# Attention in a two-layer block on one core: inverse row sums applied to the results instead of to the probability tiles

## The reference, cut to what matters

```python
probs = jax.nn.softmax(scores, axis=-1).astype(v.dtype)
out = jnp.einsum('bhcqk,bckhd->bcqhd', probs, vb)
```

## Time and profile before

| | us |
|---|---|
| median of 3 runs | 1671.91 |
| lowest, highest | 1671.36, 1674.05 |
| the profiled execution | 1673.98 |
| its span | 1671.2 |
| TensorE busy in the span | 1641.2 |
| VectorE, ScalarE, GpSimd busy | 959.7, 670.5, 156.5 |

### The profile page before, as it was taken

One profiled execution on the slowest core, in us unless ns is written; L12 is line 12 of the kernel. 1 busy time (PEld: TensorE's weight loads), 2 busy tenths in 40 slices (PEclk: granted clock), 3 DMA queues, 4 the chain that ended last, 5 costly groups with the idle time before them and its releaser, 6 DMA issues.

```text
span 1671.2 us, 20833 instructions
## 1 busy us (share of the span) xinstructions
PE 1641.2 (98%) x8516; PEld 1386.0 (83%) x8516; DVE 959.7 (57%) x1406; ACT 670.5 (40%) x1036; POOL 156.5 (9%) x230
## 2 busy tenths in 40 slices
PE   7999999999999999999999999999999999999998
PEld 6879997788888888889998887888888888888787
DVE  6755668764242434645844558544557736745757
ACT  5523365543231413523673146541334414414444
POOL 0000016300000000002720037100000000000000
PEclk9999999999999999999999999999999999999999
DMA  5221131122222222223112220322222222222331
GB/s 184 76 84 68 51 126 51 40 87 101 100 84 95 101 101 101 103 107 119 52 51 101 80 88 36 126 101 101 101 96 93 101 101 101 100 84 94 117 110 51
DMA packets 25614, 153.17 MB, mean 92 GB/s; under 512 B 3504, under 2 KB 5936, under 8 KB 8368
## 3 DMA queue, kind: packets, MB, share of 16 engines
q1 hardware_dynamic: 23184, 145.52, 24.4%
q10 hardware_dynamic: 2336, 6.33, 1.0%
HBM read 147.65 MB, written 4.19 MB: 91 GB/s over the span
## 4 chain that ended last, share of the span: by engine, by line
PE 88%; DVE 6%; ACT 2%; issue 2%; POOL 1%; DMA 0%; POOLq 0%; SPq 0%; DVEq 0%; ACTq 0%
PE bank L524 23%; PE bank L525 23%; PE bank L526 23%; PE bank L534 3%; PE bank L536 3%; PE bank L535 3%; DVE w_lo L1503 1%; PE bank L692 1%; PE bank L805 1%; PE bank L677 1%; DVE score L1626 1%; DVE row_max L1620 1%; DVE w_lo L1496 1%; PE bank L967 0%; PE bank L969 0%
## 5 line engine op out<-in xcount | busy, mean ns | idle before, releaser
L524 PE MATMUL bank<-a_hi,w_hi 128*128 128x512 f32 x1184 | 468.3, 396 | 9.3 <-DVE w_lo L1684 8.7
L526 PE MATMUL bank<-a_hi,w_lo 128*128 128x512 f32 x1184 | 462.2, 390 | 0.0
L525 PE MATMUL bank<-a_lo,w_hi 128*128 128x512 f32 x1184 | 462.0, 390 | 0.0
L1012 ACT ACTIVATE w_hi<-w_raw 128x2048 fp32r<-128x2048 f32 x120 | 229.3, 1910 | 261.3 <-DMA w_raw<-in_strips 259.6
L1496 DVE TENSOR_TENSOR w_lo<-w_raw,w_hi 128x2048 fp32r<-128x2048 f32 x117 | 267.7, 2289 | 16.4 <-ACT w_hi L1012 16.3
L524 PEld LDWEIGHTS bank<-a_hi,w_hi 128*128 128x128 f32 x1184 | 223.4, 189 | 54.3 <-DVE w_lo L1684 8.7
L526 PEld LDWEIGHTS bank<-a_hi,w_lo 128*128 128x128 f32 x1184 | 222.9, 188 | 47.1
L525 PEld LDWEIGHTS bank<-a_lo,w_hi 128*128 128x128 f32 x1184 | 223.2, 189 | 44.2 <-issue 0.2
L524 PE MATMUL bank<-b_hi,w_hi 128*128 128x512 f32 x560 | 218.2, 390 | 1.1 <-DVE w_lo L1496 0.6
L525 PE MATMUL bank<-b_lo,w_hi 128*128 128x512 f32 x560 | 217.9, 389 | 0.0
L526 PE MATMUL bank<-b_hi,w_lo 128*128 128x512 f32 x560 | 217.8, 389 | 0.0
(11 more groups left out here) (327 smaller groups left out, 2106.5 us busy)
## 6 DMA issues: line engine op xcount, KB each, us to landing
w_raw<-in_strips SPq DMA_DIRECT2D x132, 1024.0 KB, 4.8
x<-in_x_t SPq DMA_DIRECT2D x4, 512.0 KB, 7.1
head_bias<-in_rel ACTq DMA_DIRECT2D x1, 2048.0 KB, 10.6
x_kept<-x ACTq DMA_DIRECT2D x1, 2048.0 KB, 7.0
x<-x_kept SPq DMA_DIRECT2D x1, 2048.0 KB, 10.5
out<-out_t SPq DMA_DIRECT2D x12, 128.0 KB, 1.7
w_raw<-in_strips SPq DMA_DIRECT2D x4, 256.0 KB, 6.2
ws_t<-in_ws_t ACTq DMA_DIRECT2D x1, 512.0 KB, 5.6
```

Of the source, the lines that this page charges most:

```text
L524: mm(ps[:, :], w_hi[slot][:, k, cols], hi[:, k, :], start=(k == 0), stop=False)
L525: mm(ps[:, :], w_hi[slot][:, k, cols], lo[:, k, :], start=False, stop=False)
L526: return mm(ps[:, :], w_lo[slot][:, k, cols], hi[:, k, :], start=False, stop=(k == kt - 1))
L1012: run(w_hi[j], w_raw[j], ACT.Copy).then_inc(hi_split, 1)
```

## The change

`normalize` and its semaphore `normed` go, and `turn(n)` waits for `exped`. VectorE makes the reciprocals of a head's four tiles in one instruction. The row sums lie one query per partition, while the results have the queries along the row, so the inverse sums pass through a DRAM tensor `inv_kept`: ScalarE stores a head's 128 x 4 inverses as one row of 512 numbers (step 4h+4), and loads this row, repeated over 64 partitions, into half of `inv_rows` (step 4h+6, waiting for the store). GpSimd multiplies a head's result by it (`scale`), for heads 0 to 6 of a call; VectorE does it for head 7. `att_out` now counts these products, `row_added` the additions. GpSimd stages a head's copies in one go. `split_first` stands two steps later on ScalarE and VectorE.

```diff
+        inv_kept = nc.dram_tensor("inv_kept", (3 * HEADS8, T), F32, kind="Internal").ap()
+        inv_rows = sb("inv_rows", [P, T], at=work + 16896)
...
 @block.gpsimd
-                def normalize(n):
-                    w = P * (n % TT + 1)
-                    pool.wait_ge(inverted, TILE0[call] + n + 1)
-                    pool.tensor_scalar(score[:, n % 3, 0:w], score[:, n % 3, 0:w], row_inv[:, n:n + 1], 1.0,
-                                       ALU.mult, ALU.mult).then_inc(normed, 1)
-                    pool.wait_ge(normed, TILE0[call] + n + 1)
+                def scale(head):
+                    g, rows = HEAD0[call] + head, slice(HEAD * (head % 2), HEAD * (head % 2) + HEAD)
+                    dst = att_rows(call, head)
+                    pool.wait_ge(row_added, g + 1)
+                    pool.wait_ge(inv_loaded[head % 2], 16 * (g // 2 + 1))
+                    pool.tensor_tensor(dst, dst, inv_rows[rows, :], ALU.mult).then_inc(att_out, 1)
+                    pool.wait_ge(att_out, g + 1)
...
-                for part in range(COPIES[call]):
-                    stage(0, part)
-                for n in range(TILES + 1):
-                    if n:
-                        normalize(n - 1)
-                    if n < TILES - TT:
-                        for part in ((0, 1), (2, 3), (4,) if causal else (), ())[n % TT]:
-                            stage(n // TT + 1, part)
+                for head in range(HEADS8 + 2):
+                    if head < HEADS8:
+                        for part in range(COPIES[call]):
+                            stage(head, part)
+                    if 3 <= head:
+                        scale(head - 3)
 @block.tensor
                 def turn(n):
-                    pe.wait_ge(normed, t0 + n + 1)
+                    pe.wait_ge(exped, t0 + n + 1)
...
                     if head >= 2 and not second:
-                        pe.wait_ge(att_out, h0 + head - 1)
+                        pe.wait_ge(row_added, h0 + head - 1)
 @block.scalar
+                def store_inverse(head):
+                    act.wait_ge(inverted, h0 + head + 1)
+                    act.dma_start(inv_kept[h0 + head].rearrange("(t p) -> p t", p=P),
+                                  row_inv[:, TT * head:TT * head + TT], allow_slow_non_contiguous=True).then_inc(inv_stored, 16)
+                def load_inverse(head):
+                    g, rows = h0 + head, slice(HEAD * (head % 2), HEAD * (head % 2) + HEAD)
+                    act.wait_ge(inv_stored, 16 * (g + 1))
+                    if g >= 2:
+                        act.wait_ge(att_out, g - 1)
+                    act.dma_start(inv_rows[rows, :], inv_kept[g].partition_broadcast(HEAD)).then_inc(inv_loaded[head % 2], 16)
...
-                for n in range(SLOTS + 2):
+                for n in range(SLOTS + 4):
                     if 3 <= n < TILES + 3:
                         keep(n - 3)
                     if n < TILES:
                         exps(n)
-                    if n >= 8 and n % TT == 0:
+                    if 4 <= n <= TILES and n % TT == 0:
+                        store_inverse(n // TT - 1)
+                    if 6 <= n <= TILES + 2 and n % TT == 2:
+                        load_inverse((n - 6) // TT)
+                    if 8 <= n <= SLOTS and n % TT == 0:
                         copy_rows((n - 8) // TT)
-                    if not causal and n >= 9 and n % 8 == 5:
+                    if not causal and n >= 9 and n % 8 == 7:
                         split_first(n // 8 - 1)
 @block.vector
-                def invert(n):
-                    dve.wait_ge(exped, t0 + n + 1)
-                    v.reciprocal(row_inv[:, n:n + 1], row_sum[:, n:n + 1]).then_inc(inverted, 1)
+                def invert(head):
+                    mine = slice(TT * head, TT * head + TT)
+                    dve.wait_ge(exped, t0 + TT * head + TT)
+                    v.reciprocal(row_inv[:, mine], row_sum[:, mine]).then_inc(inverted, 1)
...
                     v.tensor_tensor(dst, dst, bank[6 + head % 2][HEAD * (head % 2):HEAD * (head % 2) + HEAD, :],
-                                    ALU.add).then_inc(att_out, 1)
+                                    ALU.add).then_inc(row_added, 1)
+                    if head == HEADS8 - 1:
+                        rows = slice(HEAD * (head % 2), HEAD * (head % 2) + HEAD)
+                        dve.wait_ge(row_added, h0 + HEADS8)
+                        dve.wait_ge(inv_loaded[head % 2], 16 * ((h0 + head) // 2 + 1))
+                        dve.wait_ge(att_out, h0 + HEADS8 - 1)
+                        v.tensor_tensor(dst, dst, inv_rows[rows, :], ALU.mult).then_inc(att_out, 1)
...
-                for n in range(SLOTS + 3):
+                for n in range(SLOTS + 4):
                     if n < TILES:
                         most(n)
-                    if 1 <= n < TILES + 1:
-                        invert(n - 1)
+                    if 4 <= n <= TILES and n % TT == 0:
+                        invert(n // TT - 1)
...
-                    if not causal and 9 <= n <= SLOTS + 1 and n % 8 == 5:
+                    if not causal and n >= 9 and n % 8 == 7:
                         split_first(n // 8 - 1)
```

More of the change, by code:

```diff
@@ L271, in build @@
         turned = sem("turned")
-        normed = sem("normed")
+        row_added = sem("row_added")
+        inv_stored = sem("inv_stored")
+        inv_loaded = [sem(f"inv_loaded{j}") for j in range(2)]
         p_hi_done = sem("p_hi_done")
@@ L449, in attention @@
                 causal = call != "1"
-                st, score = stage2 if causal else stage1, ATT[call]["score"]
+                st = stage2 if causal else stage1
                 def stage(head, part):
```

## The result

The changed kernel takes **1739.28 us** (median of 4 runs) beside 1672.3 us for the kernel before in the same session: ratio 1.0397, 95% interval 1.0377 to 1.0418, **slower by 67 us**. Forecast were 1665.5 us, with 1661 to 1675 as the range. Of the rivals, the one on the other side came true: the store lands late and ScalarE stands. I had given it 0.17.

What follows compares the result with a forecast made beforehand. TensorE, busy 98% of the span, was taken as the bound, with at most 11.3 us of waits to win. Terms -9.4 + 1.0 + 2.0 = -6.4 us took the 1671.91 us median to 1665.5 us; 80% range 1661 to 1675.

Steps and rivals of the forecast that it cites:

- the one on the other side: Rival: the load's wait on a late store stalls ScalarE; 1694 us at 7 us landing, 1781 at 10.6; chance 0.17.
- Part 4, the store's landing: ScalarE's load waits for the store; landing taken as 3.5 us against 4.6 us available, so no stall.
- The rival's formula: Late store's price on ScalarE: 24 x (L - 5.8) us, L being the landing time; +29 us at 7 us.
- Part 4, the issues on ScalarE's queue: 48 store and load issues on ScalarE, 0.55 us each, mostly hidden in its idle gaps: 1.0 us lost.
- Part 1: Transposes stop waiting for GpSimd's normalization: 6.9 us back in stage 1, 0.5 in 2a, 2.0 in 2b, together 9.4.
- the wait only changes its name: Rival: TensorE waits for VectorE's low parts instead; about 4 us come back, -1 us net, 1671 us; chance 0.17.
- Part 3: GpSimd's seven two-tensor products per call, 1.2 us each, replace 32 products; interference with VectorE set at nothing.
- Part 5: End of stage 1: last head's product and two more w_lo parts lengthen TensorE's wait, 2.0 us lost, wait near 2.7.

Runs made afterwards that it cites:

- e2: Changed kernel with the store writing the same 2 KB as 128 runs of 16 bytes, products then using another query's inverse: 1671.02 us.
- e8: Changed kernel storing only each head's first-tile inverses, 128 adjacent 4-byte runs; the load reads an input row, still behind the store: 1710.48 us.
- e1: Changed kernel whose load reads a row of an input and no longer waits for the store: 1684.81 us.
- e4: Changed kernel with the load of inverses one step later, at 4h+7: 1726.29 us.
- e7: Changed kernel with 16-byte-run store, strided products, stage 1's last split at step 37, and VectorE's `q_blk` staging at 4h before row addition: 1664.92 us, ratio 0.9956.
- e3: Changed kernel with the load at 4h+8 before the next store, GpSimd's product one head later, first three splits four steps later: 1720.29 us, ratio 1.0289.

## Why the prediction was wrong, point by point

**Part 4, the store's landing, is the step that failed.** The prediction had the mechanism as its rival, with its place and its formula, and dismissed it by "only a 2 KB store, on an empty queue". It sized the transfer by bytes and by queue. No row of before has 4-byte runs side by side, and their landing was taken at 3.5 us from rows of other transfers; it is 8.1 to 10.5 us in the rows above. The rival's formula, 24 x (L - 5.8), has the right order of size, and at 1.4 us (e2) nothing is lost. But it is not exact: the 9.3 us of the four rows above make it 84 us against the 68 between the change and e2, and e8's 7.8 us make it 48 against 39. It also counts the wait alone, which is 54 us (e1); held-up strips are in the 68 as well. And it fails for more time between store and load: 2.3 us more should have given back up to 55 us, e4 got 13. The range should have reached further, since both of its ends were known (1.9 and 10.6 us) and the end at 10.6 us belonged to a small transfer, 8 KB. By the Trainium skill (DMA: Bandwidth & Descriptors, "Anatomy of one DMA") the fixed cost of a DMA is about 2.0 us, given for another issuing path; e2's 1.4 us is below it, the change's 9 us far above, and the distance of the runs makes the difference.

**Part 4, the issues on ScalarE's queue**, at 1.0 us: they were a little shorter than taken (0.36 and 0.45 us instead of 0.55). e2's sum below comes out without a term for them.

**Part 1, 9.4 us back, came to about 5.** All waits of the transposes for GpSimd went. From the first scores to the last values product e2 takes 77.8 us in stage 1 where before took 80.3, so 2.5 less (forecast 6.9); it takes 0.9 less in 2a and 1.4 less in 2b (forecast 0.5 and 2.0). What the step overlooked: `turn(n)` also waits for the low part of tile n-2, because it reuses its bank. So VectorE's low part of a head's last tile holds not only the second half of the values product (L692), which I followed through, but the next transposes as well, and it stands behind the staging. This is the rival "the wait only changes its name", and nearly in its size: it had about 4 us coming back and 1671 us, and e2 took 1671.02. I had given it 0.17. That it is VectorE's order and not its load is shown by e7: the three calls are 5.4, 1.0 and 2.9 us shorter than before, together the 9.3 us that part 1 had, with VectorE's busy time in stage 1 no lower.

**Part 3, GpSimd's product beside VectorE set at nothing, was wrong in its cover.** The product's own 1.2 us was near (1.29). But its place, step 4h+9, is the very one in which VectorE stages a later head, with two inputs from SBUF: in e2 that instruction starts 0.70 us into the product and takes 1.13 instead of 0.69 us, as long as the longest of L1503, and the low part that TensorE needs is queued behind it. The rule that I had weighed (the Trainium skill, SBUF — State Buffer, "Who interferes with whom": such instructions shut each other out whole) is roughly borne out by e2's rows: the staging ends 0.55 us after the product's end at 287.80. Shut out whole, it would have ended 0.69 us after it.

**Part 5, the end of stage 1, held in its size and missed a consequence.** Forecast was a wait near 2.7 us. e2's end of stage 1 on VectorE and TensorE, which answers to the earlier trace rows:

```profile
329.74 0.69 DVE L1666 TENSOR_TENSOR qk<-qk,bank 64x512 f32<-64x512 f32 x1 [0.21 <-ACT qk L1093]
...
330.47 0.69 DVE L1673 TENSOR_TENSOR qk<-qk,inv_rows 64x512 f32<-64x512 f32 x1
...
331.19 1.90 DVE L1526 TENSOR_TENSOR w_lo<-w_raw,w_hi 128x512 fp32r<-128x512 f32 x3
...
333.00 0.68 DVE L1702 TENSOR_TENSOR b_lo<-qk,b_hi 128x512 fp32r<-128x512 f32 x1
...
333.74 0.50 PE L853 MATMUL bank<-b_hi,w_hi 128*128 128x512 f32 x1 [2.56 <-DVE b_lo L1702]
...
334.77 0.63 PE L853 MATMUL bank<-b_hi,w_hi 128*128 128x512 f32 x1
...
336.06 0.63 PE L853 MATMUL bank<-b_hi,w_hi 128*128 128x512 f32 x1
```

The wait is 2.56 us, 1.9 more than before (forecast 2.0), with the product and three parts of `w_lo` between. After it the matmuls of one kind (L853) start up to 1.29 us apart instead of 0.70: for most of four intervals TensorE works at the lower of its two clock levels. The four take 4.45 us, which costs 4.45 - 4 x 0.70 = 1.65 us. No term of the sum had that.

**The sum, put right for a store that lands**: stage 1 -2.5 + 1.9 + 1.65 = +1.05, 2a -0.9, 2b -1.4, so -1.25 us. The spans of e2 and before differ by -1.9, of which 0.4 lie ahead of stage 1. With a store that lands, the change in this order gives "no change", and the forecast of 1665.5 us was reached only by e7 with two orders changed.

## What to carry to other kernels

Before a small tensor is turned over by way of DRAM, look at how far apart the written runs lie, not only at bytes and queue: let each partition write its few numbers as one run and put them in order with a strided read on an engine. Where a wait is taken out of a loop, go through every semaphore of the waiting instruction again, reused buffers too; here the next one was an instruction queued behind something unrelated, and moving that brought the gain. And a new wait of TensorE can cost more than its own length: the 2.56 us of e2 at the end of stage 1 and the 1.8 us of e7 were followed by some 1.7 us lost at the lower clock. The length alone does not decide this: behind e2's 1.85 us at 291.01, and behind the 1.94 us of before at 302.83, the granted clock stayed at 1.00 over the next 9 us.

## What the runs showed of the hardware

- Stores of 4-byte runs side by side: 7.8 us for 128 of them and 8 to 11 for 512; 2.9 us at 8 bytes apart, 1.4 at 16, 2.1 for 512 at 64. While the slow ones are under way, a 1 MB weight strip took 17.18 us and a 128 KB load 13.19 (medians 4.8 and, beside a fast store, 2.7).
- In one such store all 528 packets had started after 1.4 us, and it landed after 9.44, with no packet of any queue starting in the 8 us between.
- The issue of the store on ScalarE's queue took 0.36 us (median of the change) and, in e3 right behind the issue of a load, 0.60 in the median and 2.33 once in stage 1. Why it was that long once is not shown.
- A strided operand (16 bytes apart) made a product of 64x512 slower on both engines: GpSimd 1.29 to 1.56 us, VectorE 0.69 to 1.08 (medians).
- The granted clock after one wait, by windows of 5 us: before (0.70 us idle), e2 (2.56 us idle), e7 (1.8 us idle):

```profile
335.00:340.00 5.00, 5.00 (x23) 4.11 (x24) 1.69 (x3) 3.11 (x4) 0.00 (x0) 1.00 0.06 26
```

```profile
335.00:340.00 5.00, 5.00 (x17) 3.99 (x17) 0.69 (x1) 0.26 (x2) 0.00 (x0) 0.73 0.00 0
```

```profile
330.00:335.00 5.00, 5.00 (x16) 3.96 (x17) 1.01 (x2) 2.39 (x3) 0.00 (x0) 0.66 0.00 0
```

17 and 16 matmuls started in 5 us where 23 did at 2.4 GHz; the windows after them show 1.00 again. Whether e7 would gain some 1.7 us more with that last wait removed was not tried.
